# Logits of two heads at once, in chunks of 512 keys, in a hybrid decoder layer's mixers

## What is computed

```python
qa, ka, va, qb, kb, vb, gate_a, gate_b = split(rmsnorm(x) @ w_in)
# A: dilated attention; query t sees key s with weight count(t, s) (how many of the patterns
#    (128,1), (512,4), (2048,16) contain s), so it is one softmax over z + log(count), causal
o_a = softmax(qa' @ ka'.T * 64**-0.5 + log(count)) @ va           # qa', ka': partial rotary
# B: stick-breaking attention, strictly causal
z = qb @ kb.T * 64**-0.5
a[t, s] = exp(log_sigmoid(z[t, s]) + sum(log_sigmoid(-z[t, j]) for s < j < t))
o_b = a @ vb
h = x + (sigmoid(gate_a) * (o_a @ w_up_a) + sigmoid(gate_b) * (o_b @ w_up_b)) @ w_out
```

## Time and profile before

| | us |
|---|---|
| Median of 3 runs (1963.29 to 1966.5) | 1964.27 |
| Profiled execution, its own time | 1963.73 |
| Its span, first to last instruction | 1961.9 |
| TensorE matmul busy | 1840.5 (94%) |
| VectorE (DVE) busy | 1121.0 (57%) |
| ScalarE (ACT) busy | 603.5 (31%) |
| GpSimd (POOL) busy | 540.1 (28%) |

### The profile page before, as it was taken

One profiled execution on the slowest core, in us unless ns is written; L12 is line 12 of the kernel. 1 busy time (PEld: TensorE's weight loads), 2 busy tenths in 40 slices (PEclk: granted clock), 3 DMA queues, 4 the chain that ended last, 5 costly groups with the idle time before them and its releaser, 6 DMA issues.

```text
span 1961.9 us, 24704 instructions
## 1 busy us (share of the span) xinstructions
PE 1840.5 (94%) x8578; PEld 1478.1 (75%) x8578; DVE 1121.0 (57%) x1684; ACT 603.5 (31%) x1024; POOL 540.1 (28%) x296
## 2 busy tenths in 40 slices
PE   5799998999899999969999889999999999999995
PEld 4577776777677777758887767888888888888884
DVE  8447884788478857886644555334333433343336
ACT  3324851476147624863212333100000000000003
POOL 5321122202211221103333103333232333233335
PEclk9899999999999999979999999999999999999998
DMA  5211111011101110135312001111111111111112
GB/s 217 100 36 38 39 56 48 29 47 55 50 28 48 52 52 29 48 122 210 128 65 86 33 12 43 54 44 44 52 48 48 43 53 43 53 43 53 43 43 86
DMA packets 43238, 118.71 MB, mean 61 GB/s; under 512 B 6160, under 2 KB 14608, under 8 KB 43024
## 3 DMA queue, kind: packets, MB, share of 16 engines
q1 hardware_dynamic: 21312, 75.66, 11.0%
q10 hardware_dynamic: 21840, 41.96, 6.3%
HBM read 97.67 MB, written 18.87 MB: 59 GB/s over the span
## 4 chain that ended last, share of the span: by engine, by line
PE 75%; DVE 13%; issue 4%; ACT 4%; ACTq 1%; POOL 1%; DMA 1%; DVEq 0%; SPq 0%; POOLq 0%
PE ps L358 64%; PE ps L472 5%; DVE e_row L1260 3%; PE ps L503 3%; PE ps L488 2%; DVE e_row L1259 2%; DVE pt L1244 1%; DVE rms L1125 1%; ACTq L801 1%; DVE raw L1158 1%; POOL rms L339 1%; ACT pt L843 1%; DVE h L1468 1%; DVE raw L1174 1%; ACT n_hi L969 0%
## 5 line engine op out<-in xcount | busy, mean ns | idle before, releaser
L324 POOL TENSOR_SCALAR w_hi<-w_stage 128x1024 fp32r<-128x1024 f32 x138 | 150.5, 1090 | 1390.5 <-issue 687.7
L358 PE MATMUL ps<-n_hi,w_hi 128*128 128x512 f32 x1536 | 402.4, 403 | 24.6 <-DVE raw L1158 13.8
L358 PE MATMUL ps<-n_lo,w_hi 128*128 128x512 f32 x1536 | 391.2, 395 | 0.0
L358 PE MATMUL ps<-n_hi,w_lo 128*128 128x512 f32 x1536 | 388.2, 393 | 0.0
L326 POOL TENSOR_TENSOR w_lo<-w_stage,w_hi 128x1024 fp32r<-128x1024 f32 x138 | 368.2, 2668 | 11.5
L358 PEld LDWEIGHTS ps<-n_hi,w_hi 128*128 128x128 f32 x1536 | 290.2, 192 | 93.5 <-DVE raw L1158 19.9
L358 PEld LDWEIGHTS ps<-n_lo,w_hi 128*128 128x128 f32 x1536 | 289.1, 190 | 60.6
L358 PEld LDWEIGHTS ps<-n_hi,w_lo 128*128 128x128 f32 x1536 | 285.4, 188 | 58.1
L1328 DVE TENSOR_TENSOR h<-ps,h 128x512 f32<-128x512 f32 (+1 forms) x192 | 132.1, 691 | 155.4 <-PE ps L358 155.0
L1024 ACT ACTIVATE a_hi<-u_f 128x1024 fp32r<-128x1024 f32 x22 | 23.4, 1062 | 475.3 <-DVE u_f L1434 475.3
L1426 DVE TENSOR_TENSOR u_f<-ps,rms 128x512 f32<-128x512 f32 x44 | 30.4, 692 | 205.3 <-PE ps L358 205.3
(11 more groups left out here) (168 smaller groups left out, 2213.5 us busy)
## 6 DMA issues: line engine op xcount, KB each, us to landing
w_stage<-weights_in SPq DMA_DIRECT2D x138, 512.0 KB, 3.2
gates_scratch<-raw ACTq DMA_DIRECT2D x16, 512.0 KB, 2.8
o_scratch<-o_sum ACTq DMA_DIRECT2D x128, 32.0 KB, 1.8
n_lo<-o_scratch ACTq DMA_DIRECT2D x8, 512.0 KB, 5.2
g_a<-gates_scratch ACTq DMA_DIRECT2D x8, 512.0 KB, 3.6
g_b<-gates_scratch ACTq DMA_DIRECT2D x8, 512.0 KB, 4.4
h<-x_t_in ACTq DMA_DIRECT2D x8, 512.0 KB, 9.0
out_t<-h ACTq DMA_DIRECT2D x16, 256.0 KB, 2.1
```

The costliest lines, as they stand in the source:

```text
L324: pool.tensor_scalar(w_hi[:, b, :], stage[:, b, :], 1.0, 1.0, ALU.mult, ALU.mult).then_inc(w_rounded, 1)
L358: ins = pe.matmul(bank, w[:, b, c:c + P], mv(k), start=(first and n == 0), stop=(last and n == total - 1))
```

## The change

A slot's logits are now those of both heads of a query block, for one chunk of at most 512 keys, head 0 in bank 2 and head 1 in bank 3, the matmuls of the two heads alternating. `chunk(s)` gives the keys: units s and s+1 of a pair share a query block; the even slot takes the last chunk (with the diagonal), the odd slot the first 512 keys if there are more than 512, else nothing. So 24 of 32 slots have logits. The next logits wait for the reads of both heads' chunks. In A, DVE reads head 0's chunk at the slot's head and head 1's after pt_lo; the maximum is carried over the chunks, and scaling and reciprocal are done once for both heads; both Exps follow in the slot that completes the pair. In B, ACT copies and Abs, Exp, Ln run per chunk and head, DVE's chain runs per chunk with a scan that starts from a carry copied out of the chunk before, and the final Exp still takes a whole row, in the slot two after the completing one.

```diff
+def chunk(s):
+    width = (ORDER[s][1] + 1) * P
+    parts = [(c, min(HALF, width - c)) for c in reversed(range(0, width, HALF))]
+    return parts[s % 2] if s % 2 < len(parts) else None
+
+def completes(s):
+    return 0 <= s < UNITS and (s % 2 == 1) == (ORDER[s][1] >= HALF // P)
...
-                def logits(u):
+                def logits(s):
...
-                    if u:
-                        pe.wait_ge(logits_free, base + u)
-                    for c in range(0, width, HALF):
-                        for n, (a, b) in enumerate(((q_hi, k_hi), (q_hi, k_lo), (q_lo, k_hi))):
-                            ins = pe.matmul(ps[:, 2 + c // HALF, 0:w], a[hs, blk(qb)], b[hs, c:c + w],
...
+                    if s:
+                        pe.wait_ge(logits_free, i * READS + READ[s])
+                    c, w = chunk(s)
+                    for n, (a, b) in enumerate(((q_hi, k_hi), (q_hi, k_lo), (q_lo, k_hi))):
+                        for h in range(2):
+                            hs = slice(h * HD, (h + 1) * HD)
+                            ins = pe.matmul(ps[:, 2 + h, 0:w], a[hs, blk(qb)], b[hs, c:c + w],
...
 ACT, slot s
+                def scaled(s, h):
+                    act.activation(rows[:, u % 4, c:c + w], ps[:, 2 + h, 0:w], ACT.Copy, scale=HD ** -0.5
+                                   ).then_inc(logits_free, 1)
+                def weights_of(u):
+                    act.activation(row, row, ACT.Exp).then_inc(pB_ready, 1)
...
+                    if completes(s - 2) and s - 2 >= 16:
+                        weights_of((s - 2) // 2 * 2)
+                    if s >= 16 and s in READ:
+                        scaled(s, 0)
...
+                    if s >= 16 and s in READ:
+                        scaled(s, 1)
+                    if completes(s - 2) and s - 2 >= 16:
+                        weights_of((s - 2) // 2 * 2 + 1)
+                    if s < 16 and completes(s):
+                        act.wait_ge(max_ready, i * 8 + (s // 2 + 1))
+                        for u in (s // 2 * 2, s // 2 * 2 + 1):
+                            act.activation(row, row, ACT.Exp, scale=HD ** -0.5, bias=stat[:, 1, c:c + 1],
+                                           accum_out=stat[:, 2, c:c + 1]).then_inc(exp_ready, 1)
+                    if s >= 16 and s in READ:
+                        e = [e_row[:, h, c:c + w] for h in range(2)]
...
+                            act.activation(e[h], rows[:, (s // 2 * 2 + h) % 4, c:c + w], ACT.Abs).then_inc(act_step, 1)
...
+                            act.activation(e[h], e[h], ACT.Exp, scale=-1.0).then_inc(act_step, 1)
...
+                            act.activation(e[h], e[h], ACT.Ln, bias=1.0).then_inc(soft_ready, 1)
 DVE
+                def biased(s, h):
+                    dve.tensor_tensor_reduce(
+                        out=rows[:, u % 4, c:c + w], in0=ps[:, 2 + h, 0:w], in1=bias_A[:, at:at + w], scale=1.0,
+                        scalar=top if s % 2 else NEG_MAX, op0=ALU.add, op1=ALU.max, accum_out=top
+                    ).then_inc(logits_free, 1)
+                def remaining(s):
+                    for h in range(2):
+                        link(dve.scalar_tensor_tensor(e, row, 0.0, e, ALU.max, ALU.add))
+                        link(dve.tensor_tensor_scan(e[:, ::-1], e[:, ::-1], e[:, ::-1], carry if s % 2 else 0.0,
+                                                    ALU.add, ALU.bypass))
+                        if not completes(s):
+                            link(dve.tensor_copy(carry, e[:, 0:1]))
+                        dve.tensor_tensor(row, row, e, ALU.subtract).then_inc(arg_ready, 1)
 DVE, slot s
+                    if s < 16 and s in READ:
+                        biased(s, 0)
...
+                    if s < 16 and s in READ:
+                        biased(s, 1)
+                    if s < 16 and completes(s):
+                        dve.tensor_scalar(stat[:, 1, c:c + 2], stat[:, 0, c:c + 2], -HD ** -0.5, None, ALU.mult
+                                          ).then_inc(max_ready, 1)
+                    if s - 1 < 16 and completes(s - 1):
+                        link(dve.reciprocal(stat[:, 3, c:c + 2], stat[:, 2, c:c + 2]))
+                        for u in (first, first + 1):
+                            dve.tensor_scalar(row, row, stat[:, 3, u % 4:u % 4 + 1], None, ALU.mult).then_inc(pA_ready, 1)
+                    if s - 1 >= 16 and s - 1 in READ:
+                        remaining(s - 1)
```

More of the change, by code:

```diff
@@ L57 @@
 SLOTS = UNITS + 4
+def chunk(s):
[4 more added lines that the diff above has]
+    return 0 <= s < UNITS and (s % 2 == 1) == (ORDER[s][1] >= HALF // P)
+CHUNKS = [s for s in range(UNITS) if chunk(s)]
+READ = {s: 2 * n for n, s in enumerate(CHUNKS)}
+READS = 2 * len(CHUNKS)
+READS_A = READ[16]
+READS_B = READS - READS_A
+EARLIER = {s: max(r for r in CHUNKS if 16 <= r < s and chunk(r)[0] == chunk(s)[0]) for s in CHUNKS if s >= 18}
 class Plan:
@@ L855, in round_ @@
+                    if completes(s - 2) and s - 2 >= 16:
[3 more added lines that the diff above has]
+                        for u in (s // 2 * 2, s // 2 * 2 + 1):
+                            row = rows[:, u % 4, 0:(ORDER[u][1] + 1) * P]
                             c = u % 4
-                            act.wait_ge(max_ready, i * 16 + (u + 1))
                             act.activation(row, row, ACT.Exp, scale=HD ** -0.5, bias=stat[:, 1, c:c + 1],
@@ L858, in round_ @@
                                            accum_out=stat[:, 2, c:c + 1]).then_inc(exp_ready, 1)
-                        else:
-                            e = e_row[:, u % 2, 0:width]
-                            act.wait_ge(logits_free, base + (u + 1))
-                            act.activation(e, rows[:, u % 4, 0:width], ACT.Abs).then_inc(act_step, 1)
-                            act.wait_ge(act_step, i * 32 + (STEPS_ACT + 2 * (u - 16) + 1))
-                            act.activation(e, e, ACT.Exp, scale=-1.0).then_inc(act_step, 1)
-                            act.wait_ge(act_step, i * 32 + (STEPS_ACT + 2 * (u - 16) + 2))
-                            act.activation(e, e, ACT.Ln, bias=1.0).then_inc(soft_ready, 1)
+                    if s >= 16 and s in READ:
+                        c, w = chunk(s)
+                        e = [e_row[:, h, c:c + w] for h in range(2)]
+                        n = i * (2 * READS_B) + (STEPS_ACT + 2 * (READ[s] - READS_A))
+                        for h in range(2):
+                            act.wait_ge(logits_free, i * READS + (READ[s] + h + 1))
+                            if s >= 18:
+                                act.wait_ge(arg_ready, i * READS_B + (READ[EARLIER[s]] - READS_A + h + 1))
+                            act.activation(e[h], rows[:, (s // 2 * 2 + h) % 4, c:c + w], ACT.Abs).then_inc(act_step, 1)
+                        for h in range(2):
+                            act.wait_ge(act_step, n + (h + 1))
+                            act.activation(e[h], e[h], ACT.Exp, scale=-1.0).then_inc(act_step, 1)
+                        for h in range(2):
+                            act.wait_ge(act_step, n + (h + 3))
+                            act.activation(e[h], e[h], ACT.Ln, bias=1.0).then_inc(soft_ready, 1)
@@ new lines, in remaining @@
+                def remaining(s):
+                    c, w = chunk(s)
+                    for h in range(2):
+                        u = s // 2 * 2 + h
+                        row, e = rows[:, u % 4, c:c + w], e_row[:, h, c:c + w]
+                        carry = stat[:, 2, u % 4:u % 4 + 1]
+                        dve.wait_ge(soft_ready, i * READS_B + (READ[s] - READS_A + h + 1))
+                        link(dve.scalar_tensor_tensor(e, row, 0.0, e, ALU.max, ALU.add))
[4 more added lines that the diff above has]
+                        dve.tensor_tensor(row, row, e, ALU.subtract).then_inc(arg_ready, 1)
```

93 lines of the change are left out of this document (33 added, 60 removed).

## The result

| | before | after |
|---|---|---|
| Median of the comparison's runs, us | 1963.87 (1963.29 to 1966.5) | 2023.78 (2022.55 to 2026.04) |
| Ratio | | 1.0306, 95% interval 1.0293 to 1.0319 |
| Profiled execution's span, us | 1961.9 | 2021.9 |

The change makes the kernel 59.9 us (3.1%) slower. The forecast was slower by 10, and 2023.8 lies outside its range: the sign was right, the size was not.

A forecast was written before the change was run, and what follows sets the result against it. TensorE was taken to bound the rounds except mixer B's wide slots, where DVE does. Terms -3.6 + 1.9 + 6.0 - 1.7 = +2.6 us a round, +10.4 over four rounds, gave 1974.5 us, range 1940 to 2000.

The forecast's parts named there:

- A narrow: Mixer A, slots 0 to 8: TensorE is full, so fewer logits blocks save 3.6 us a round.
- A wide: Mixer A, slots 9 to 15: a new loop through the second head's read adds 1.9 us a round.
- B wide: Mixer B, slots 16 to 24: DVE sets the end and its split rows add 6.0 us a round.
- B narrow: Mixer B, slots 25 to 35: half of TensorE's saving from fewer blocks arrives, 1.7 us a round.
- The overlap of the halves: Logits matmuls on rows 0 to 63 and 64 to 127 run at once; six of 512 take about 0.88 us.
- the rival without overlap alone: The two heads' matmuls don't overlap: 8.3 us a round longer, 1997 us; 18%.
- The reading of slot 21: B's slot 21: TensorE waits 2.2 us for DVE's raw read, taken as DVE setting the end of wide slots.
- the loop: A's wide slots: next logits wait for the second read, behind pt_lo, pt_hi and transposes; slot 14 takes 5.3 us.
- ACT's share: B's wide slots: ACT's split operations add 6.4 us a round, mostly covered; 0.4 us taken for the later first chain.
- The step that failed: B's wide slots: even units' transposes come a slot later; TensorE waits about 1 us in odd slots, covered by DVE.
- TensorE's relief at the end: Rival: the loop doesn't bind, idle DVE absorbs work, narrow B gives all; 8.3 us a round shorter, 1931 us; 27%.

The follow-up runs named there:

- run 3: Changed kernel with head 0's three matmuls first and a semaphore wait before head 1's first logits matmul; 2064.79 us, ratio 1.0519.
- run 4: Changed kernel with DVE's read of head 1's chunk in mixer A moved early, ahead of the o work or pt_lo; 2013.7 us, ratio 1.0251.
- run 5: Kernel before, with only DVE's chain of mixer B cut at 512 keys with a carried scan; 1983.87 us, ratio 1.01.
- run 6: Kernel before, with DVE's chain and ACT's copy, Abs, Exp and Ln of mixer B cut at 512 keys; 1984.59 us, ratio 1.0104.
- run 1: Changed kernel with B's narrow slots alternating the halves of e_row, using its spare half; 2009.64 us, ratio 1.022.
- run 9: Changed kernel with pairs only in mixer A (early second read) and B from slot 26; slots 16 to 25 as before; 1962.63 us, ratio 0.9994.
- run 11: Changed kernel with pairs in mixer A alone and the early second read, all of B as in the kernel before; 1956.52 us, ratio 0.9959.
- run 8: Changed kernel with the spare half of e_row, the early second read, and wide pairs taking 512 keys first, the remainder second; 1985.8 us, ratio 1.0117.
- run 12: As run 11, with A's wide rows taking the chunk of 512 keys first and the remainder second; 1945.63 us, ratio 0.9907.

## Why the prediction was wrong, point by point

Per round, in us, beside the lengths of the second round:

| step | predicted | measured |
|---|---|---|
| A narrow, slots 0 to 8 | -3.6 | -3.8 |
| A wide, 9 to 15 | +1.9 | +3.7 |
| B wide, 16 to 23 (predicted with slot 24) | +6.0 | +7.7 |
| slots 24 and 25 | within the two beside it | +7.3 |
| B narrow, the rest | -1.7 | 0.0 |
| sum | +2.6 | +14.9 |

- **The overlap of the halves**: right, 0.89 us for six as priced. The narrowest blocks were overpriced: six 128-wide matmuls were put at 0.85 us, and slot 8's takes 0.47 (363.67 to 364.14). With a semaphore between the halves it is 41 us more (run 3); this holds the handover too, so it doesn't price the rival without overlap alone, which was put at 23 more than the forecast.
- **The reading of slot 21** The earlier trace rows set 3.22 us of matmuls against 1.68 us of weight loads. The like of it, eight matmuls at the upper clock, is 2.09. And between a DVE scan that POOL held for 2 us (the rows stand under the hardware below) and the `raw` read that ends the wait of 2.16 us, DVE works without a gap; the prediction took all of DVE's busy time for its own work.
- **A narrow**: right, 3.8 for 3.6.
- **A wide**: mechanism right, term mis-sized, +3.7 for +1.9. Slot 14 was priced at 5.3 and took 5.14. But slots 10 and 11 took 3.0 us more, where the prediction has -0.2 for the one and no figure for the other, behind a scaling held for 1.86 us by POOL, which the sum doesn't have. The early read ends the loop (slots 9 and 12 to 15 are 2.9 us below the kernel before, run 4) and leaves the hold.
- **B wide, DVE's extra work**: right. 4.8 us a round alone (run 5), and in the changed kernel DVE is busy 52.02 us in slots 16 to 23 against 46.84, +5.2. ACT's share beside it: right for the kernel before with ACT's cuts, nothing (run 6). What the step left out is that the stretch grew by 2.5 us more than DVE's work, so DVE is less full after (52 of 62.6 us, 83%) than before (85%).
- **The step that failed**, by 7.3 of the 12.3 us a round that the sum lacks, is the sentence on the even unit's transposes, "makes TensorE wait about 1 us in odd slots, under the same cover". Three rows of the odd wide slots show what it is, the last with what stands behind such a wait:

```profile
427.69 1.97 PE L510 MATMUL ps<-ident,rows 128*128 128x128 f32 x8 [2.52 <-ACT rows L862]
445.00 0.98 PE L510 MATMUL ps<-ident,rows 128*128 128x128 f32 x7 [1.37 <-ACT rows L862]
447.26 3.60 PE L378 MATMUL ps<-n_hi,w_hi 128*128 128x512 f32 x8 [1.28 <-DVE raw L1198]
```

  It was priced for wide slots alone and as covered. In slot 25 the same wait is 6.56 us, since ACT stands ahead of it for `e_row`; over the run it is 49.9 us. The prediction followed the queues through DVE and ACT but never asked, buffer by buffer, which slot's data each write replaces. `EARLIER[24]` is 23, and that is in the code of the change. Undoing this reuse alone took 7.2 us a round out of its place (run 1) and 14 us out of the time.
- **B narrow**: taken as half of TensorE's saving. The pairing itself costs there (6.1 us between runs 9 and 11), and this eats the saving.
- **The rivals**: TensorE's relief at the end, 27%, was true of A's narrow slots; A's wide slots came below the kernel before only by the early read. None of the rivals had a wait of ACT for a buffer.
- **The sum** by its own terms is 1974.1 and 0.5 more, 1974.6 or 1974.7 and not 1974.5, which changes nothing.

What stays open. Of B's 56 us (2023.8 less 1967.9), 19 are DVE's cut chains and 14 are `e_row`, net. The other 23 are not taken apart: the narrow pairing is some 6 of them, and waits for the final Exp in odd wide slots are in the trace, but no run removed these (run 8's order of chunks left the stretch as long). Nor is it settled why slots 16 to 23 take 2 us more wherever A runs in pairs. Deeper `rows` or `e_row` buffers for all of B were not tried, and neither was POOL's split at another place.

## What to carry to other kernels

When a change alters how a buffer is cut, list for every slot which earlier slot's data it overwrites; the one place where the distance falls from two slots to one can cost more than all added work (7.3 of 14.9 us a round here). Look also for an operation that is much longer than its like: a share of busy time hides that it stood behind another engine. Cut a round at its slots and compare the stretches: the busy shares of the whole page moved by 4 points and named nobody. And apply a change only where the engine it relieves sets the end: the paired logits in mixer A alone, with the second read early and the short chunk last, are 0.9% faster than the kernel before, 0.4% of it without the order of the chunks and the luck in it (runs 11 and 12); in both mixers they are 3.1% slower.
